# Second block's projections and copies reordered, first layer's output gates computed beside the last transforms

## What is computed

```python
def second_block(x, mem, ...):
    for l in range(DEPTH):
        y = hybrid_mixer(x, w_in[l], cmp_pe[l], ...)
        x = layer_norm(DN_ALPHA * x + y, ln_g[l, 0], ln_b[l, 0])
        y = memory_cross_attention(x, mem, xa_w_q[l], xa_w_kv[l], xa_w_o[l])
        x = layer_norm(DN_ALPHA * x + y, ln_g[l, 1], ln_b[l, 1])
        y = jnp.square(jax.nn.relu(x @ mlp_w_up[l])) @ mlp_w_down[l]
        x = layer_norm(DN_ALPHA * x + y, ln_g[l, 2], ln_b[l, 2])

def hybrid_mixer(h, w_in, ...):
    (nq, nkc, nvc, nks, nvs, nkw, nvw, ngate,
     cq, ckv, kr, fq, fk, fv, ff) = jnp.split(h @ w_in, split_points, axis=-1)
    o_nsa = nsa_attention(nq, nkc, nvc, nks, nvs, nkw, nvw, ngate, ...)  # ngate: sigmoid gates
    o_mla = mla_attention(cq, ckv, kr, q_norm, w_uq, kv_norm, w_ukv)     # latent norm, then w_uq, w_ukv
    o_fox = fox_attention(fq, fk, fv, ff, b_f)                           # cumsum(log_sigmoid(ff + b_f))
    ...
```

## Time and profile before

| | us |
|---|---|
| median of three runs | 3161.57 |
| lowest, highest | 3159.11, 3167.48 |
| profiled execution, device time | 3164.42 |
| its span in the trace | 3162.6 |

### The profile page before, as it was taken

The page is one execution under the profiler, slowest core; times in us unless marked ns, Lnnn a source line. Parts: engine busy times, 40 slices in busy tenths (PEclk is TensorE's granted clock), DMA queues, the critical chain, the costliest instruction groups (busy, mean ns, idle before and its releaser), DMA issues.

```text
span 3162.6 us, 43506 instructions
## 1 busy us (share of the span) xinstructions
PE 2917.9 (92%) x17412; PEld 2338.2 (74%) x17412; DVE 1667.8 (53%) x3180; ACT 1068.7 (34%) x1871; POOL 447.0 (14%) x401
## 2 busy tenths in 40 slices
PE   5889999998997899899999899999899999899998
PEld 2478774688984477476888689898566688779988
DVE  6855657754577743845235542426564433563334
ACT  3333335224135531634222431322353422332231
POOL 3200003231004520303020000000131111000000
PEclk8999999999998999899999999999899999999999
DMA  5433220222233034021332332323211233133231
GB/s 169 147 125 103 84 87 1 80 79 94 68 90 65 26 104 101 1 62 47 100 99 87 101 94 94 93 94 78 67 42 34 74 100 111 57 100 101 83 104 67
DMA packets 245423, 262.00 MB, mean 83 GB/s; under 512 B 12818, under 2 KB 227970, under 8 KB 245096
## 3 DMA queue, kind: packets, MB, share of 16 engines
q1 hardware_dynamic: 227808, 203.93, 21.4%
q0 software_dynamic: 12544, 45.08, 4.1%
q10 hardware_dynamic: 4872, 10.21, 1.5%
HBM read 245.04 MB, written 13.11 MB: 82 GB/s over the span
## 4 chain that ended last, share of the span: by engine, by line
PE 56%; DVE 9%; issue 2%; ACT 2%; DMA 0%; POOL 0%; DVEq 0%; SPq 0%; ACTq 0%; POOLq 0%
PE PS L346 30%; PE PS L3705 10%; PE PS L156 3%; PE PS L1154 3%; PE PS L1167 2%; PE PS L1178 2%; PE PS L3604 2%; DVE S L1205 2%; DVE S L1233 1%; DVE HL L294 1%; DVE S L2591 1%; DVE S L2587 1%; DVE S L1226 1%; ACT HL L287 1%; PE PS L3366 1%
## 5 line engine op out<-in xcount | busy, mean ns | idle before, releaser
L346 PE MATMUL PS<-xT,HL 128*128 128x512 f32 (+2 forms) x3552 | 797.0, 386 | 12.5 <-DVE xT L2443 4.7
L294 DVE TENSOR_TENSOR HL<-S,HL 128x2048 fp32r<-128x2048 f32 (+1 forms) x204 | 423.1, 2079 | 676.1 <-ACT HL L287 676.1
L346 PEld LDWEIGHTS PS<-xT,HL 128*128 128x128 f32 (+1 forms) x3552 | 648.5, 189 | 153.9 <-DVE xT L2443 5.4
L287 ACT ACTIVATE HL<-S 128x2048 fp32r<-128x2048 f32 (+1 forms) x204 | 351.4, 1729 | 702.3 <-PE PS L346 277.4
L3705 PE MATMUL PS<-HL,hd 128*128 128x256 f32 x3072 | 370.2, 283 | 0.1
L3705 PEld LDWEIGHTS PS<-HL,hd 128*128 128x128 f32 x3072 | 369.4, 190 | 0.8 <-PE PS L3705 0.5
L1264 ACT ACTIVATE S<-S,S 128x256 f32<-128x256 f32 (+5 forms) x292 | 189.2, 648 | 211.5 <-DVE S L1205 204.2
L1299 POOL TENSOR_SCALAR S<-S,S 128x512 f32<-128x512 f32 (+4 forms) x104 | 178.8, 1719 | 406.5 <-DVE S L1220 236.9
L1167 PEld LDWEIGHTS PS<-S,S 128*128 128x128 f32 (+1 forms) x1048 | 115.7, 143 | 144.9 <-issue 40.0
L1167 PE MATMUL PS<-S,S 128*128 128x128 f32 (+1 forms) x1048 | 172.4, 292 | 42.6 <-DVE S L1233 15.4
L346 PE MATMUL PS<-h_high,HL 128*128 128x512 f32 (+1 forms) x768 | 202.8, 350 | 0.1
(11 more groups left out here) (406 smaller groups left out, 3939.7 us busy)
## 6 DMA issues: line engine op xcount, KB each, us to landing
S<-in_mlp_w_up SPq DMA_DIRECT2D x32, 1024.0 KB, 5.6
S<-in_mlp_w_down SPq DMA_DIRECT2D x32, 1024.0 KB, 5.1
S<-in_w_in SPq DMA_DIRECT2D x28, 1024.0 KB, 5.2
S<-in_w_ada SPq DMA_DIRECT2D x24, 1024.0 KB, 5.1
S<-in_w_gate SPq DMA_DIRECT2D x24, 1024.0 KB, 5.2
S<-in_w_in SPq DMA_DIRECT2D x36, 512.0 KB, 5.2
S<-in_w_mix_out SPq DMA_DIRECT2D x8, 1024.0 KB, 5.7
spectra<-S POOLq DMA_DIRECT2D x24, 256.0 KB, 4.8
```

Source lines behind the costliest of these rows:

```text
L287: m = a.activation(high, raw, ACT.Copy)
L294: m = v.tensor_tensor(low, raw, high.bitcast(F32), ALU.subtract)
L346: m = pe.matmul(dst, l[x], r[y], start=(i == 0 and j == 0), stop=(i == n - 1 and j == 2))
```

## The change

Five edits.

1. `gates(0, GB)` is called before the barrier, right behind the last inverse transforms, instead of after `hyena_gate`. All four copies are ACT's (`on_v=False`), and the gates lie in UC's columns 512 to 1023 of four token tiles, whose reader has finished.
2. In both layers of the second block the `kp` projection comes before `compressed(0)`, and the narrow projection between `compressed(0)` and `compressed(1)`; the two chunks change places in the list.
3. In both layers the `vv` projection comes before `narrow_turn` and `branch_gates`, which now stand last before the barrier.
4. In both layers `forget_logs` is written behind the transposes and copies of the normed latents instead of ahead of them.
5. The gates' destination is a list of halves. `gates` now has a parameter `on_v`, and its loop assigns to a variable of that name: with the default, the first turn asks `dve_turn()` and the second finds the name set.

```diff
-                 [(1280, 1304), (1816, 1848), (2616, 2620)], [(768, 896), (1024, 1152)], [(896, 1024), (1152, 1280)]]
+                 [(768, 896), (1024, 1152)], [(1280, 1304), (1816, 1848), (2616, 2620)], [(896, 1024), (1152, 1280)]]
...
-    def gates(l, dst):
+    def gates(l, dst, on_v=None):
...
-            b, on_v = bank(), dve_turn()
+            b, on_v = bank(), dve_turn() if on_v is None else on_v
...
+    GB = [[UC[:, t, 512:1024] for t in ts] for ts in ((0, 1), (2, 5))]
+    gates(0, GB, False)
     f = barrier()
     tx = load_x(f)
...
     hyena_gate()
-    GB = [sb(BIG + 12800, 1024), sb(BIG + 13824, 1024)]
-    gates(0, GB)
...
-    gates(1, GB)
+    gates(1, [[GB[0][:, 0:512], GB[0][:, 512:1024]]])
...
         gx1, t_gx1 = hidden(1)
+        project3_T([(i * 128, 128, [(kp[:, i, :], 0, 128)]) for i in range(2)])
+        compressed(0, gx0, t_gx0)
         t_narrow = project3_T([(0, 60, [(narrow[0:60, :], 0, 60)])])
-        compressed(0, gx0, t_gx0)
-        project3_T([(i * 128, 128, [(kp[:, i, :], 0, 128)]) for i in range(2)])
         compressed(1, gx1, t_gx1)
+        project3(xT, range(4), 256, lambda t: [(vv[:, t, :, :].rearrange("p b c -> p (b c)"), 0, 256)])
         narrow_turn()
         branch_gates()
-        project3(xT, range(4), 256, lambda t: [(vv[:, t, :, :].rearrange("p b c -> p (b c)"), 0, 256)])
         f = barrier()
...
         project3_T([(j * 128, 128, [(fq[:, j, :], 0, 128)]) for j in range(2)], scale=-0.125)
-        t_ll = forget_logs()
         pe.wait_ge(*t_cq)
         transposed([([cq[:, t, k * 128:k * 128 + 128] for t in range(4)], [(cT_[:, k, :], 0, 128)]) for k in range(4)])
         t_cT = evac_token()
+        t_ll = forget_logs()
```

More of the change, by code:

```diff
@@ L567, in dve @@
                     v.wait_ge(*full)
-                    v.tensor_copy(dst[c][:, h * 512:h * 512 + 512], PS[:, b, :]).then_inc(*vl.event())
+                    v.tensor_copy(dst[c][h], PS[:, b, :]).then_inc(*vl.event())
         def act():
@@ L573, in act @@
                     a.wait_ge(*full)
-                    a.activation(dst[c][:, h * 512:h * 512 + 512], PS[:, b, :], ACT.Copy).then_inc(*al.event())
+                    a.activation(dst[c][h], PS[:, b, :], ACT.Copy).then_inc(*al.event())
         tensor()
@@ L963, in dve @@
                         v.wait_ge(*added_by[at - 2])
-                    v.tensor_tensor(tmp[at % 2], PS[:, b, 0:256], GB[0 if t < 4 else 1][:, n * 256:n * 256 + 256], ALU.mult
+                    v.tensor_tensor(tmp[at % 2], PS[:, b, 0:256], GB[0 if t < 4 else 1][n // 2][:, n % 2 * 256:n % 2 * 256 + 256], ALU.mult
                                     ).then_inc(*vl.event())
@@ L2457, in program @@
     g.tensor_copy(gates1, GB[0]).then_inc(*gl.event())
-    out_proj(yT, parts, 4, [gates1], t_y, grid(AREA + 12288, 2, 256), turned=True,
+    out_proj(yT, parts, 4, [[gates1[:, 0:512], gates1[:, 512:1024]]], t_y, grid(AREA + 12288, 2, 256), turned=True,
              moved=[moved, ld_scr.all()])
```

## The result

The changed kernel takes **3141.35 us** (median of 4 runs, 3138.49 to 3143.54), measured beside 3164.53 us for the kernel before (4 runs, 3159.11 to 3173.37); the ratio is 0.9924, 95% interval 0.9897 to 0.995. Faster by 0.8%, as forecast, and within half a microsecond of the forecast time. Two later comparisons of the same kernel gave 0.9943 (0.993 to 0.9957) and 0.9959 (0.9943 to 0.9974). Over all runs the medians are 3144.3 us (17 runs) and 3161.2 us (86 runs), so -17 us rather than -20.9.

A forecast was written before the change was run, and what follows sets the result against it. PE was taken to bound the kernel, by its idle time and slow clock at five places. Gates -3.1, key waits -7.9 and clock -3.7, narrow turn +1.4, logs -4.9 and clock -4.3, turns +1.6: -20.9, so 3141 us (3134 to 3151).

The forecast's parts named there:

- the forecast time: Whole kernel: 3141 us, the median of 3161.6 us less the summed 20.9 us; chance 0.58.
- the slow stretch behind it: Second block, both layers: full clock behind the shortened waits, saving 3.7 us at compressed keys and 4.3 us at latent projections.
- A price for a load: Second block: kp chunk's load taken at 9.5 us (other row 11.1 us), so no PE wait in front of kp.

## What to carry to other kernels

When an edit is worth 3 us and the untouched start of the same program scatters by 8, compare stretches between landmarks over several traces, and time each part both alone and left out. A wait removed in front of dense matmuls also gave back the slow stretch behind it in most executions (17 of 18 and 13 of 18 here), but look at what comes next, for the clock can be lost again there. A price for a load should be taken from the row with the same loads ahead of it in the queue, and a variable named like a parameter can reorder a whole schedule.

## What the runs showed of the hardware

The time at half speed differs between executions of one program: 65 to 85 us up to the first barrier, and 154 to 188 us over the whole of three traces of the changed kernel (191 and 201 us in two of the kernel before). The spans of those three follow it: 3136.6, 3142.8 and 3148.8 us with 154, 181 and 188 us.

The clock fell in the middle of work without a pause. 64 score matmuls of 64 rows by 32 columns, PE busy for 6.18 of 6.20 us, ran at a mean granted clock of 0.56, behind an idle time of 1.17 us, while behind 0.56 us the group took 3.76 us at a granted clock of 1.00 in some executions and up to 5.36 us in others. Against drops in the middle of a kernel, the Trainium skill (TensorE: Matmul & The Clock Gate, Why this matters for your kernels) asks for short idle gaps between bursts of matmuls. Here the clock fell with gaps of 0.56 and 1.17 us, so that alone does not keep it up. The same section's row on thin-M matmuls ties such falls to DMAs between the K-tiles, and PE waited for nothing among these 64.

The kp chunk is two loads of 512 KB, issued behind the two loads of 512 KB of `cmp_w1` on one queue. Its split could start 11.2 to 13.1 us after the first of the four was issued (18 layers). In layer 0 of the trace after, kp's two loads landed 8.6 and 8.7 us behind their own issues, while the page's median for loads of this kind and size, from issue to landing, is 5.2 us:

```profile
S<-in_w_in SPq DMA_DIRECT2D x36, 512.0 KB, 5.2
```
